# Two transformer blocks on one core: both sums of a double norm from one x, other orders at the second feed-forward stage, and gated heads' logarithms earlier

## What is computed

```python
def first_block(x, ...):
    u = rmsnorm(h, norm_mix_w); proj = u @ w_in
    f = lb + (1 - lb) * sigmoid(hf); log_f = log(f); k = 1 - f      # 4 gated heads of 128
    o_hg = rmsnorm(hgrn2_chunkwise(q, k, v, log_f), hg_norm_w) * silu(hg)
    o_att = sliding_window_attention_with_sinks(aq, ak, av, sinks)
    h = h + concatenate([o_hg, o_att]) @ w_out
    v = rmsnorm(h, norm_ffn_w)
    h = h + (silu(conv(v @ w_gate)) * (v @ w_up)) @ w_down
    return rmsnorm(h, final_norm_w)
def second_block(x, mem, ...):
    h = rms_norm(x, mix_pre_g); z = h @ w_in                         # pooling, fox attention, gates
    x = x + rms_norm(merged @ w_mix_out, mix_post_g)
    x = x + rms_norm(mem_attention(rms_norm(x, xa_pre_g), mem_n, ...), xa_post_g)
    x = x + rms_norm(conv_ffn(rms_norm(x, ffn_pre_g), ...), ffn_post_g)
```

## Time and profile before

| | |
|---|---|
| median of 3 runs | 2959.22 us (2953.76 to 2959.88) |
| the profiled execution | 2952.08 us |
| its span | 2950.3 us |
| mean granted clock of TensorE | 0.98 |
| TensorE busy | 2822.5 us, 96% |
| VectorE, ScalarE, GpSimd busy | 43%, 27%, 33% |
| the chain that ended last | TensorE 81%, VectorE 11%, ScalarE 4% |

### The profile page before, as it was taken

One profiled execution on the slowest core, in us unless ns is written; L12 is line 12 of the kernel. 1 busy time (PEld: TensorE's weight loads), 2 busy tenths in 40 slices (PEclk: granted clock), 3 DMA queues, 4 the chain that ended last, 5 costly groups with the idle time before them and its releaser, 6 DMA issues.

```text
span 2950.3 us, 35148 instructions
## 1 busy us (share of the span) xinstructions
PE 2822.5 (96%) x13902; PEld 2306.8 (78%) x13902; DVE 1270.2 (43%) x1792; ACT 800.0 (27%) x1237; POOL 967.6 (33%) x1007
## 2 busy tenths in 40 slices
PE   7899998999999999998999998999979999999998
PEld 6888785888888888877797776777657888888886
DVE  4355537433322232255404444348476334443436
ACT  5244427221001011134113334234452111111114
POOL 3622310743333333332422110355124333433330
PEclk9999999999999999999999999999989999999999
DMA  5422230411111111125544232532012111111103
GB/s 213 149 98 93 100 108 23 143 57 58 56 43 57 43 43 57 33 26 105 131 98 104 79 108 73 185 105 97 29 49 94 43 57 43 43 43 43 58 28 114
DMA packets 156933, 230.59 MB, mean 78 GB/s; under 512 B 5284, under 2 KB 116239, under 8 KB 156823
## 3 DMA queue, kind: packets, MB, share of 16 engines
q1 hardware_dynamic: 110448, 136.85, 16.0%
q10 hardware_dynamic: 46375, 92.24, 8.9%
HBM read 181.33 MB, written 47.74 MB: 78 GB/s over the span
## 4 chain that ended last, share of the span: by engine, by line
PE 81%; DVE 11%; ACT 4%; issue 2%; DMA 1%; ACTq 0%; POOL 0%; DVEq 0%; POOLq 0%
PE PS L830 30%; PE PS L297 21%; PE PS L843 10%; PE PS L1169 4%; PE PS L2212 2%; PE PS L1175 2%; PE PS L857 2%; PE PS L1226 2%; PE PS L1857 2%; DVE SC L590 1%; PE PS L1899 1%; PE PS L1927 1%; PE PS L1915 1%; DVE SC L972 1%; DVE SC L975 1%
## 5 line engine op out<-in xcount | busy, mean ns | idle before, releaser
L2829 POOL CAST wh<-raw 128x512 fp32r<-128x512 f32 (+1 forms) x488 | 332.6, 696 | 1898.5 <-issue 1186.7
L2833 POOL TENSOR_TENSOR wl<-raw,wh 128x512 fp32r<-128x512 f32 (+1 forms) x488 | 659.7, 1362 | 0.0
L297 PE MATMUL PS<-UH,wh 128*128 128x512 f32 x1040 | 426.0, 410 | 36.8 <-DVE UL L680 16.8
L297 PE MATMUL PS<-UH,wl 128*128 128x512 f32 x1040 | 408.2, 393 | 0.0
L297 PE MATMUL PS<-UL,wh 128*128 128x512 f32 x1040 | 408.2, 393 | 0.0
L830 PE MATMUL PS<-UL,wh 128*128 128x512 f32 x1280 | 394.2, 389 | 0.0
L830 PE MATMUL PS<-UH,wl 128*128 128x512 f32 x1280 | 394.0, 389 | 0.0
L830 PE MATMUL PS<-UH,wh 128*128 128x512 f32 x1280 | 394.0, 389 | 0.0
L830 PEld LDWEIGHTS PS<-UH,wl 128*128 128x128 f32 x1280 | 240.2, 188 | 50.0
L830 PEld LDWEIGHTS PS<-UL,wh 128*128 128x128 f32 x1280 | 240.2, 188 | 50.0
L830 PEld LDWEIGHTS PS<-UH,wh 128*128 128x128 f32 x1280 | 240.2, 188 | 49.8
(11 more groups left out here) (326 smaller groups left out, 3994.1 us busy)
## 6 DMA issues: line engine op xcount, KB each, us to landing
raw<-in_w_up SPq DMA_DIRECT2D x33, 1024.0 KB, 7.1
raw<-in_w_in SPq DMA_DIRECT2D x27, 1024.0 KB, 10.3
raw<-in_w_down SPq DMA_DIRECT2D x22, 1024.0 KB, 5.0
raw<-in_w_gate SPq DMA_DIRECT2D x11, 1024.0 KB, 5.3
raw<-in_w_out SPq DMA_DIRECT2D x8, 1024.0 KB, 6.1
xres<-XT ACTq DMA_DIRECT2D x4, 2048.0 KB, 7.1
zgate<-SC ACTq DMA_DIRECT2D x32, 256.0 KB, 2.1
SC<-zgate ACTq DMA_DIRECT2D x16, 512.0 KB, 4.9
```

Of the source, the lines that this page charges most:

```text
L297: mm = pe.matmul(PS[:, banks[f], :], w[:, k, f * P:(f + 1) * P], u[:, k, half(h)], start=(k == 0 and j == 0), stop=(k == n_k - 1 and j == 2))
L2829: pool.tensor_copy(wh[slot][:, cols], raw[slot % 2][:, cols]).then_inc(hi_done[slot], 1)
L2833: low = pool.tensor_tensor(wl[slot][:, cols], raw[slot % 2][:, cols], wh[slot][:, cols].bitcast(F32), ALU.subtract)
```

## The change

It has three parts.

In First, the logarithm of head h + 1 is issued in step 8 of head h, ahead of the evacuation that stands there. For head 0 the loads of f and q are issued at evacuation 2 and the logarithm at 4 (before 5 and 7); f stays in the place where its logarithm goes.

In FFN1's tail, ScalarE squares each tile twice, once with the weight of the final norm, and VectorE adds up both. TensorE sums both next to each other. ScalarE gets the second norm's factor from the two sums with a chain of two logarithms and three exponentials, with a multiplication and an addition of VectorE in it; the two weights are multiplied once. The splits of half 0 stand among the additions of half 1; the renewal of x and its stores come after the splits.

At the end of Chain and in FFN2's head, the last scores are turned earlier, the renewals of half 0 start at step 16, high parts and output tiles alternate, banks and waits of output tiles differ, and the second sum of half 1 is made by TensorE: eight products with ones, one per squared tile, in place of seven additions and one product. The head waits by slots.

Instructions in all: 3 rows more on TensorE (7 products with ones more), one table load and two activations more on ScalarE, two instructions fewer on VectorE.

```diff
-                if (h, pos, k) == (0, 0, 2):
-                    self.add_up(pe, 1, 0)
-                if (h, pos, k) == (0, 1, 5):
-                    self.add_up(pe, 1, 1)
+                if (h, pos, k) == (0, 0, KT - 1):
+                    self.add_up_both(pe, 1)
...
+            def beside(self, pe, h, slot, k):
+                if (h, slot, k) == (0, 0, 5 if self.on_tensor else 2):
+                    self.add_up(pe, 1, 0)
+                if self.on_tensor and (h, slot) == (0, 1) and k < 4:
+                    self.total(pe, 2 * k)
+                    self.total(pe, 2 * k + 1)
+            def total(self, pe, k):
+                pe.wait_ge(*self.sq[1](KT + k + 1))
+                mm = pe.matmul(PS[:, self.banks[1][1], :], ones[:], self.buf(k % 2, 1), start=k == 0, stop=k == KT - 1)
+                mm.then_inc(self.sums[1].sem if k == KT - 1 else self.totals.sem, 1)
...
+            def add_up_both(self, pe, h):
+                self.add_up(pe, h, 0)
+                pe.wait_ge(*self.acc2[h](KT - 1))
+                pe.matmul(PS[:, self.banks[h][1], :], ones[:], self.buf(3, h), start=True, stop=True).then_inc(self.sums[h].sem, 1)
+            def rstd_both(self, act, h):
+                self.logarithm(act, h, 0)
+                act.wait_ge(*self.sums[h](2))
+                act.wait_ge(*self.ln[h](1))
+                act.activation(self.buf(3, h), self.buf(2, h), ACT.Exp, scale=-1.0).then_inc(self.inverse[h].sem, 1)
+                self.root(act, h, 0)
+                act.wait_ge(*self.ms[h](1))
+                act.activation(self.buf(3, h), PS[:, self.banks[h][1], :], ACT.Ln, bias=eps, scale=1.0 / D).then_inc(self.ln[h].sem, 1)
+                act.wait_ge(*self.both[h](1))
+                act.activation(PS[:, self.banks[h][1], :], self.buf(2, h), ACT.Exp, scale=-0.5).then_inc(self.rstd_ready[h].sem, 1)
+            def second_square(self, dve, h):
+                dve.wait_ge(*self.inverse[h](1))
+                bank = PS[:, self.banks[h][1], :]
+                dve.tensor_tensor(bank, bank, self.buf(3, h), ALU.mult).then_inc(self.ms[h].sem, 1)
+            def add_logarithms(self, dve, h):
+                dve.wait_ge(*self.ln[h](2))
+                dve.wait_ge(*self.rstd_ready[h](1))
+                dve.tensor_tensor(self.buf(2, h), self.buf(2, h), self.buf(3, h), ALU.add).then_inc(self.both[h].sem, 1)
+            def join_weights(self, dve):
+                (t, at, n), (t2, at2, _) = (PCOL[name] for _, name in self.phases)
+                w, w2 = prm[:, t, at:at + n], prm[:, t2, at2:at2 + n]
+                dve.tensor_tensor(w2, w2, w, ALU.mult).then_inc(self.joined_weights.sem, 1)
...
+            def rstd_at(self, h, p):
+                if self.phases[p][0] in ("turned", "scale"):
+                    return self.buf(0 if self.double else 5, h)
+                return PS[:, self.banks[h][p], :]
...
-                pe.wait_ge(*self.before)
                 for h in range(2):
                     for slot, full in ((0, self.g_full), (1, self.u_full)):
+                        if h == 0 and slot < len(self.before):
+                            pe.wait_ge(*self.before[slot])
                         if h == 0:
...
-                            for phase, at in enumerate(self.sums_at):
-                                if at == (h, slot, k):
-                                    self.norm.add_up(pe, 1, phase)
+                            self.norm.beside(pe, h, slot, k)
...
+                    if m == 1 and not self.second:
+                        self.then.add_up_both(pe, 0)
                     part(1, m, 1, 4 + m % 4).then_inc(self.y_full.sem, 1)
-                    if m == 1:
+                    if m == 1 and self.second:
                         self.then.add_up(pe, 0, 0)
...
+                act.wait_ge(*then.joined_weights(1))
                 for m in range(KT):
                     act.wait_ge(*self.y_free(self.added + m + 1))
-                    then.square(act, 0, 0, m, XT[:, m, half(0)])
+                    then.square_both(act, 0, m)
+                then.rstd_both(act, 0)
+                highs = {1: (0, 1), 2: (2,), 3: (3,), 4: (4,), 5: (5,), 7: (6, 7)}
...
+                    then.square_both(act, 1, m)
+                    then.high(act, 0, highs.get(m, ()))
+                then.rstd_both(act, 1)
                 then.keep(act, 0)
-                then.rstd(act, 0, 1)
-                then.high(act, 0, range(KT))
-                then.rstd(act, 1, 0)
-                then.squares(act, 1, 1, range(KT))
+                then.high(act, 1, range(KT))
                 then.keep(act, 1)
-                then.rstd(act, 1, 1)
-                then.high(act, 1, range(KT))
...
+                then.join_weights(dve)
+                for m in range(KT):
+                    add_half(m, 0, (m + 4) % 8)
+                    if m >= 1:
+                        then.accumulate_both(dve, 0, m - 1)
+                then.accumulate_both(dve, 0, KT - 1)
+                splits = {2: (0, 1), 3: (2,), 4: (3,), 5: (4,), 6: (5,)}
+                sums = {2: (1,), 3: (2,), 4: (3,), 5: (4,), 6: (5,)}
+                for m in range(KT):
+                    add_half(m, 1, 4 + m % 4)
+                    if m == 1:
+                        then.second_square(dve, 0)
+                    if m == 2:
+                        then.add_logarithms(dve, 0)
+                    then.split(dve, 0, splits.get(m, ()))
+                    for k in sums.get(m, ()):
+                        then.accumulate_both(dve, 1, k)
+                for k in (6, 7):
+                    then.accumulate_both(dve, 1, k)
+                then.split(dve, 0, (6, 7))
+                dve.wait_ge(*then.lo[0](KT))
+                then.renew(dve, 0, (0, 1), sums=False)
+                then.second_square(dve, 1)
+                then.renew(dve, 0, range(2, 6), sums=False)
+                then.add_logarithms(dve, 1)
+                then.renew(dve, 0, (6, 7), sums=False)
                 then.split(dve, 1, range(KT))
+                dve.wait_ge(*then.lo[1](KT))
+                then.renew(dve, 1, range(KT), sums=False)
...
+                def logarithm(h):
+                    act.wait_ge(*self.fk(h * 2 + 1))
+                    act.wait_ge(*(self.mr(h * LEVELS) if h else self.fk(2)))
+                    act.activation(self.E[0], self.F if h else self.E[0], ACT.Ln).then_inc(self.lnf.sem, 1)
...
+                    if n == 2:
+                        load(self.KE, zf1[0:P, :], self.f_loaded, "f0")
+                        load_rows(self.q, zq1, 0, self.q_loaded, "q")
+                    if n == 4:
+                        logarithm(0)
                     if n == 5:
                         for j in range(2):
                             act.wait_ge(*self.zst[j](uses[j]))
-                        load(self.KE, zf1[0:P, :], self.f_loaded, "f0")
-                        load_rows(self.q, zq1, 0, self.q_loaded, "q")
                         load_values(0)
-                    if n == 7:
-                        act.wait_ge(*self.fk(1))
-                        act.activation(self.E[0], self.F, ACT.Ln).then_inc(self.lnf.sem, 1)
...
+                        if p == 8 and h + 1 < HG:
+                            logarithm(h + 1)
                         if p:
                             next(evacuated)
...
-                        dve.tensor_scalar(self.F, self.f if h else self.KE, omlb[:, h:h + 1], lb[:, h:h + 1], ALU.mult, ALU.add).then_inc(self.fk.sem, 1)
+                        F = self.F if h else self.E[0]
+                        dve.tensor_scalar(F, self.f if h else self.KE, omlb[:, h:h + 1], lb[:, h:h + 1], ALU.mult, ALU.add).then_inc(self.fk.sem, 1)
                         dve.wait_ge(*self.fk(h * 2 + 1))
-                        dve.tensor_scalar(self.k, self.F, -1.0, 1.0, ALU.mult, ALU.add).then_inc(self.fk.sem, 1)
+                        dve.tensor_scalar(self.k, F, -1.0, 1.0, ALU.mult, ALU.add).then_inc(self.fk.sem, 1)
...
-                        pe.wait_ge(*norm.sq[1](t - 5))
+                        pe.wait_ge(*(norm.sq[1](2) if t == 6 else norm.xn[0](KT)))
...
+                    if s == 16:
+                        self.turn(pe, 15)
                     self.between(pe, s)
                     if s == 14:
                         self.joined.add_up(pe, 0, 0)
-                    if 1 <= s <= 16:
+                    if 1 <= s <= 15:
...
+                    if s == 16:
+                        turned(7)
+                    if s < 16:
+                        probs(s)
                     if s == 15:
                         joined.rstd(act, 0, 0)
-                    if s < 16:
-                        probs(s)
...
-                    joined.squares(act, 0, 1, {16: (0,), 17: (1,), 18: (2, 3)}.get(s, ()))
-                renewed = {0: (4,), 1: (5, 6, 7)}
-                for t in range(KT):
+                    joined.squares(act, 0, 1, {17: (0, 1), 18: (2, 3)}.get(s, ()))
```

(39 more changed lines are left out.)

107 lines of the change are left out of this document (64 added, 43 removed).

## The result

The change is faster: **2929.25 us** median (2926.06 to 2936.45, 5 runs), where the kernel before took 2958.93 (2953.76 to 2959.88, 5 runs) beside it. The ratio is 0.9909, with 0.9893 to 0.9925 as its 95% interval, so 22 to 32 us off, 26.9 by the ratio (29.7 by the medians). The profiled execution took 2929.25 us, span 2927.1; that is 23 us under the profiled execution of before, which lay some 7 us under its own median.

A forecast was written before the change was run, and what follows sets the result against it. TensorE, busy 96% of the span, was taken as the bound, leaving its matmul work, waits and slow clock. Terms -8.0 - 4.5 - 7.1 - 2.0 = -21.6 against the 2959.2 median gave 2938 us, range 2926 to 2952.

The forecast's parts named there:

- gated heads: Gated heads' masked operands: earlier logarithms and scans remove 8.0 us of TensorE's idle time, and the clock gives 4.5 more.
- boundary: End of the first feed-forward stage: TensorE waits 7.2 us where it waited 14.3, so -7.1, between -10.6 and -4.5.
- chain and second head: Chain's end and second feed-forward head: first piece +1.6, second piece -3.6, net -2.0 us, between +8 and -6.
- Head 0: First gated head: counted at nothing, its shorter wait against scans moved into GpSimd's splitting; bounds -1.5 and +3 us.
- Heads 1 to 3: Later gated heads: logarithm ahead of the evacuation removes waits of 3.3 us (heads 1 and 2) and 4.74 (head 3).
- clock term: Gated heads: matmuls at the lower clock speed up once waits are short; 4.5 us taken between 0 and 5.2.
- rival F: A table load in a chain holds ScalarE 1.4 us beyond its 1.28: boundary -3.0, 2942 us; chance 0.01.
- B: More than forecast: boundary -10.6 without contention, heads' clock -5.2, chain -6; about -30 us, so 2929; chance 0.15.
- A: Clock stays low, GpSimd eats more: gated heads -6, boundary -4.5, chain +1.5; -9 us, so 2950; chance 0.17.
- E: The change doesn't do what it says, because something else is late at each place: 2956 us; chance 0.02.
- C: Chain loses: second head's ones-matmuls at half speed, 14 us for eight, VectorE later; chain +8, whole -12, 2947; chance 0.08.
- D: Slower: the second feed-forward head stays at the lower clock throughout, costing 29 us more, so 2967; chance 0.03.

The follow-up runs named there:

- the late split: The changed kernel, but GpSimd holds the split of the second pooling weight until half 0's sixth low part is there: 2928.24 us, ratio 0.9897.

## Why the prediction was right and where it was wrong

It said 2938, in 2926 to 2952, and faster at 0.94. Faster and the range held; the figure was 8.8 us too high. By the stretches, with the means over the traces of all kernels that have a part old and of those that have it as in the change (heads 3 and 8 traces, boundary 3 and 9, chain 3 and 6):

```
                       forecast   measured
gated heads               -12.5      -18.2   (445.6 to 427.4)
boundary                   -7.1       -7.8   (677.7 to 669.9)
chain and second head      -2.0       -1.4   (132.0 to 130.6)
sum                       -21.6      -27.4
```

Counted from the first L297 product, which leaves out the scatter ahead of it, the heads gave -18.8 (416.0 to 397.1). The chain's -1.4 is hardly outside its own scatter: the old part took 131.5 to 132.7 us, the new one 130.3 to 131.7.

**Head 0: the step that failed.** "Head 0 I count at nothing" stood on scans that move into the time of GpSimd's splits. They moved ahead of it. In the changed kernel (timelines of VectorE and ScalarE):

```profile
109.80 2.63 DVE L1730 TENSOR_TENSOR_SCAN XT<-ones,XT 128x128 f32<-128x128 f32 x8 [2.91 <-ACT XT L1510]
```

```profile
139.17 1.28 ACT L1548 ACT_TABLE_LOAD   x1 [2.22 <-DMA mv<-SC]
```

and in the kernel before:

```profile
127.95 7.92 DVE L1617 TENSOR_TENSOR_SCAN XT<-ones,XT 128x128 f32<-128x128 f32 x8 [8.07 <-ACT XT L1415]
```

```profile
140.78 1.28 ACT L1435 ACT_TABLE_LOAD   x1 [6.11 <-DMA mv<-SC]
```

The scans are over at 112.4, where GpSimd begins at 112.13; before, they ran at 127.95 beside it and took 7.92 instead of 2.63. The excess that I set as the upper bound of the harm was already in the kernel before, and fell away. GpSimd did pay: its first block took 10.1 us (112.13 to 122.19) where it had taken 7.2 (111.08 to 118.25), and TensorE waited 4.57 for it, where it had waited 1.68 and 2.10 for this block and the next. So the new wait for weights, which I had named as a sign of being wrong, did come, at 122.29. But the wait at the masks and the clock behind it went, and the run with head 0 old puts the net gain at 6.9 us on average, and at 2.7 at the least, outside the bounds of -1.5 and +3.

The reason that I gave for those 2 us is wrong as well: "its exponentials no longer stand behind a store and its landing". They still do. In all nine traces with head 0 as changed, ScalarE's load ahead of the first exponential waited 2.2 to 2.3 us for the landing of the store mv, while the differences that it needs had been ready for some 25 us (VectorE's row in this trace ends at 114.39). In the kernel before, the differences were ready at 138.52 and the same landing came 2.2 us later; in the three other traces with head 0 old, the differences came last. So the early scans took VectorE out of this chain, and what is left in it is the store. The start of the scans should have been worked out from the chain (f loaded at evacuation 2, logarithm at 4) instead of from where the splits stand.

**Heads 1 to 3** were right in mechanism. Of 4.74 at head 3, 0.66 stayed, since the operations behind the scan met GpSimd: the scan took 2.63, the operation behind it at 332.35 2.28 against 1.22 at head 1. The clock term was taken at 4.5 of 5.2: 3.2 of its 3.6 at head 3 showed in the run with the old order there, and no L1309 of the changed kernel took over 2 us. With 7.2 us for head 3 and 6.9 for head 0, heads 1 and 2 gave 18.8 - 6.9 - 7.2 = 4.7, against 3.3 + 1.6 = 4.9; with the 8.3 by which head 3 was longer in the three kernels that have all heads old, 3.6. The 1.6 rested on one trace: head 1's L1201 ran at the lower clock in one of these three, head 2's in another, neither in the third.

**The boundary** was right nearly to the term. Predicted waits 0.9, 0.4 and 5.9, measured 0.72, 0.40 and 5.77; half 1, counted as free by a margin of 1.5, kept 0.33. Contention was put at 3.5. Here is VectorE beside GpSimd's splits, in the changed kernel:

```profile
1308.42 1.10 DVE L667 TENSOR_TENSOR SC<-SC 128x512 f32<-128x512 f32 x1
1309.44 1.77 DVE L617 TENSOR_TENSOR SC<-SC 128x512 f32<-128x512 f32 x1
1311.14 0.68 DVE L1099 TENSOR_TENSOR XT<-PS,XT 128x512 f32<-128x512 f32 x1
1311.74 0.73 DVE L693 SCALAR_TENSOR_TENSOR SC<-PS,prm,XT 128x512 f32<-128x512 f32 x1
1312.40 1.09 DVE L761 TENSOR_TENSOR UL<-SC,UH 128x512 fp32r<-128x512 f32 x1
```

Two of these steps lost 0.42 us and one 1.10, while the two that read PSUM lost nothing; with the four more to 1317.80 the losses sum to 3.9, and the late split took 3.2 of the wait away. ScalarE's chain of two logarithms and three exponentials, in the changed kernel:

```profile
1288.64 0.69 ACT L675 ACTIVATE SC<-PS,small 128x512 f32<-128x512 f32 x1 [0.44 <-PE PS L671]
1289.40 1.28 ACT L629 ACT_TABLE_LOAD   x1
1290.70 0.63 ACT L629 ACTIVATE SC<-SC 128x512 f32<-128x512 f32 x1
1291.24 0.62 ACT L679 ACTIVATE SC<-SC 128x512 f32<-128x512 f32 x1
1291.87 1.28 ACT L632 ACT_TABLE_LOAD   x1
1293.16 0.69 ACT L632 ACTIVATE SC<-PS,small 128x512 f32<-128x512 f32 x1
1293.87 1.28 ACT L634 ACT_TABLE_LOAD   x1
1295.17 0.60 ACT L634 ACTIVATE PS<-SC 128x512 f32<-128x512 f32 x1
```

From the sums' start at 1287.48 to its end at 1295.77 are 8.3 us, against 8.0. Each load stands between its neighbours with under 0.1 us beside its own 1.28. So rival F is refuted for this chain, which VectorE waits for. The Trainium skill (ScalarE: Activation LUTs, What ACT_TABLE_LOAD costs) states a drain of about 1.38 us on top of a load; it does not appear here, at any of the three loads.

**The chain** came out at -1.4, near the forecast of -2.0, by errors that cancel: that is luck. First piece, from the start of the first wait to half 0's second sum: forecast 24.6, measured 2151.81 - (2127.31 - 3.02) = 27.5, so +4.5 and not +1.6. I had left GpSimd out: its split of a block, which before stood behind VectorE's renewals (from 2165.71), ran from 2139.25 to 2148.3 amid them. VectorE's timeline there:

```profile
2142.80 1.65 DVE L698 TENSOR_TENSOR XT<-SC,XT 128x512 f32<-128x512 f32 x1
2144.38 1.09 DVE L667 TENSOR_TENSOR SC<-SC 128x512 f32<-128x512 f32 x1
...
2147.07 1.74 DVE L667 TENSOR_TENSOR SC<-SC 128x512 f32<-128x512 f32 x1
```

where such a step takes 0.68 alone; five of them lost 3.8 us. The first wait was 3.02 and not 1.6, so the wait at the sum came out at 10.0, as forecast (9.7), from a TensorE and a VectorE both later. The second piece, to half 1's first product of the head, took 45.9 us (2151.81 to 2197.70), where before it took 51.0: -5.1 and not -3.6 (my own terms, -5.4 and two microseconds of slow clock, give -3.4; the sum has -3.6). Its waits were 0.26, 0.47 and 2.55 for the 4.5 counted, and the ones-matmuls cost 0.86 each for 0.87. The lower clock behind the 10 us wait ended after some 3 us (matmuls at 0.23 us again from 2154.90) and cost 1.5; behind the wait of 2.55 it came back for another 3.4 us (TensorE's matmuls at half speed from 2175.46 to 2178.89) and cost 1.6. I had counted 4.5. The window there:

```profile
2175.00:2179.00 4.00, 3.54 (x9) 2.82 (x10) 3.96 (x7) 0.83 (x2) 0.00 (x0) 0.57 0.00 0
```

In the second trace of the same kernel the same wait, 2.57, left the clock at 1.00. The two pieces sum to -0.6; the stretch gave -1.4 because another +0.4 lies ahead of them and -1.3 behind, where half 1's wait of 4.86 is gone and nothing follows it at half speed. The prediction had no term for either.

**The rivals.** B gave the time, 2929, but not its way: of its three parts only the heads' clock came; the boundary met contention and the chain did not give 6. A is refuted by the heads, which gave 18 and not 6, and E with it. C and D are refuted: the granted clock is 1.00 throughout the second head but for the 3.4 us above, and its eight ones-matmuls ran at 0.86 us. Of the 8.8 us, 5.8 stand in the table; the other 3 are in no stretch that the change touches and within the interval of the ratio.

## What to carry to other kernels

A wait can cost more than its length: behind each of the gated heads' waits of 4.6 to 7.4 us TensorE ran at the lower clock for some microseconds, and at head 3 removing the wait gave both back. Before contention is priced, work out from its own inputs where a moved step will stand against the other engines' heavy stretches: it may leave one that it was in (head 0) or meet one that nobody named (the chain's renewals). Where a change leaves one long wait in front of a sum, look at the sum's inputs and at the sums behind it: here TensorE made the sum, another moved two places up, and the chain gave 4 us more.
